# Three sample stages rewritten: index scores by pairs of batches, forget scores and values in column tiles, rings of caches, unrolled loops

## The reference, cut to what matters

```python
# index scores (8 heads of 64 share one key of 64): group A keeps its top 256 keys by them
dots  = einsum('bthd,bsd->bths', iq, ik_all) * 64 ** -0.5
score = einsum('bth,bths->bts', iw * 8 ** -0.5, relu(dots))
sel_score, sel = top_k(score, 256)
# group A: 8 heads on 2 KV heads, softmax over the selected keys with a bias by position
# group B, "forget" attention: 8 heads with keys of their own
logits = einsum('bthd,bshd->bhts', q, k_all) * 64 ** -0.5
logits = logits + (f_q[..., :, None] - f_k[..., None, :])   # cumulative sums of log forget
out    = einsum('bhts,bshd->bthd', softmax(mask(logits)), v_all)
```

## Time and profile before

| | us |
|---|---|
| median of 3 executions (4905.27 to 4925.78) | 4916.42 |
| the profiled execution, its own time | 4921.45 |
| its span in the trace | 4919.4 |
| the index stage, from 2258 to 2460 of the span | 202 |
| the forget stage, 2460 to 2892 | 432 |
| the sparse stage, 2892 to 3093 | 201 |

### The profile page before, as it was taken

The page is one execution under the profiler, slowest core; times in us unless marked ns, Lnnn a source line. Parts: engine busy times, 40 slices in busy tenths (PEclk is TensorE's granted clock), DMA queues, the critical chain, the costliest instruction groups (busy, mean ns, idle before and its releaser), DMA issues. The chain is left out here.

```text
span 4919.4 us, 56872 instructions
## 1 busy us (share of the span) xinstructions
PE 4268.2 (87%) x20062; PEld 3271.9 (67%) x20062; DVE 2392.9 (49%) x4716; ACT 2009.3 (41%) x3516; POOL 188.4 (4%) x224
## 2 busy tenths in 40 slices
PE   7997979997577888898789967797999999999998
PEld 6897967776334444442244535687989898989887
DVE  5322247776587777851134522343434352525354
ACT  4111126665576777752222312223334242424243
POOL 0000000000110000000000000010000000000000
PEclk9998989998688889897689978898999999999999
DMA  4344353331411010001165447565444354444454
GB/s 135 100 135 122 118 151 78 78 78 34 109 49 44 24 39 20 20 7 28 29 205 190 141 109 147 165 204 175 154 137 168 127 169 135 146 155 151 148 163 146
DMA packets 478509, 557.84 MB, mean 113 GB/s; under 512 B 95433, under 2 KB 388177, under 8 KB 473981
## 3 DMA queue, kind: packets, MB, share of 16 engines
q1 hardware_dynamic: 461122, 497.73, 33.3%
q0 software_dynamic: 17120, 56.65, 4.0%
HBM read 444.45 MB, written 109.83 MB: 113 GB/s over the span
## 5 line engine op out<-in xcount | busy, mean ns | idle before, releaser
L2199 DVE TENSOR_TENSOR w_lo<-w_raw,w_hi 128x2048 fp32r<-128x2048 f32 x192 | 440.2, 2293 | 643.3 <-ACT w_hi L2164 629.2
L2164 ACT CAST w_hi<-w_raw 128x2048 fp32r<-128x2048 f32 x192 | 366.7, 1910 | 568.1 <-PE ps_y L2149 541.1
L2128 PE MATMUL ps_u<-h_hi,w_hi 128*128 128x384 f32 (+1 forms) x1536 | 505.9, 329 | 48.9 <-DMA h_lo<-h2lo 27.0
L2130 PE MATMUL ps_u<-h_hi,w_lo 128*128 128x384 f32 (+1 forms) x1536 | 503.4, 328 | 0.0
L2129 PE MATMUL ps_u<-h_lo,w_hi 128*128 128x384 f32 (+1 forms) x1536 | 503.3, 328 | 0.0
L2147 PE MATMUL ps_y<-w_hi,hid_hi 128*128 128x512 f32 x1088 | 423.5, 389 | 0.6 <-DVE w_lo L2199 0.4
L2149 PE MATMUL ps_y<-w_hi,hid_lo 128*128 128x512 f32 x1088 | 423.4, 389 | 0.0
L2148 PE MATMUL ps_y<-w_lo,hid_hi 128*128 128x512 f32 x1088 | 423.3, 389 | 0.0
L332 PE MATMUL ps_u<-hT_hi,wi_hi 128*128 128x436 f32 (+1 forms) x920 | 341.7, 371 | 46.7 <-DVE o_lo L494 29.9
L334 PE MATMUL ps_u<-hT_hi,wi_lo 128*128 128x436 f32 (+1 forms) x920 | 335.9, 365 | 0.0
L333 PE MATMUL ps_u<-hT_lo,wi_hi 128*128 128x436 f32 (+1 forms) x920 | 335.7, 365 | 0.0
(11 more groups left out here) (261 smaller groups left out, 8209.7 us busy)
## 6 DMA issues: line engine op xcount, KB each, us to landing
w_raw<-in_w_up SPq DMA_DIRECT2D x96, 1024.0 KB, 5.3
w_raw<-in_w_down SPq DMA_DIRECT2D x96, 1024.0 KB, 4.9
k_rows_b<-in_cache_b_k SPq DMA_DIRECT2D x32, 1024.0 KB, 11.9
v_rows_b<-in_cache_b_v SPq DMA_DIRECT2D x32, 1024.0 KB, 5.3
part_hi<-o_hi SPq DMA_DIRECT2D x68, 218.0 KB, 2.0
part_lo<-o_lo SPq DMA_DIRECT2D x68, 218.0 KB, 2.2
wi_raw<-in_w_in SPq DMA_DIRECT2D x18, 512.0 KB, 4.3
mx<-mixed SPq DMA_DIRECT2D x17, 512.0 KB, 6.5
```

The lines of the kernel that those rows point to most:

```text
L2128: pe.matmul(out, w_hi[s][:, c], h_hi[:, k, 0:w], start=(k == 0), stop=False)
L2130: mm = pe.matmul(out, w_lo[s][:, c], h_hi[:, k, 0:w], start=False, stop=(k == KD - 1))
L2164: act.copy(w_hi[i % 2][:, :], raw[i % RAW][:, :]).then_inc(ev("w_hi"), 1)
L2199: nc.vector.tensor_tensor(w_lo[i % 2][:, :], raw[i % RAW][:, :], w_hi[i % 2][:, :].bitcast(FP32), ALU.subtract)\
```

## The change

Four things are done, all in the two functions. `need` and the hardware loops go: the batches are written out one by one.

*Index stage.* Two batches form a pair. Their keys lie side by side in one tile, so one transposition turns both; the first batch's keys come to partitions 0 to 63 and the second's to 64 to 127, and the two score products of a chunk use the two halves of TensorE's rows and two PSUM banks. The second product writes 32 columns at partition 0, 32, 64 or 96 (a column tile). All small loads for the 8 batches, 27 DMAs, come ahead of the first score. The keys of each pair have a tile of their own. The forget sums are taken after the third pair and are stored in two parts, high and low, as float32r.

The second batch's queries and mask are now issued after two quarters of the first batch's values, no longer behind all of them. The diff, cut to its core:

```diff
 def sample_index_phase(nc, ctx, d):
...
-        kT = sb("ikT_s", [HD, LS])
+        kn = [sb(f"ik_rows{i}", [P, NBLK, 2, HD]) for i in range(NPR)]
+        kT = [sb(f"ikT_s{i}", [P, PAST]) for i in two]
...
+            def score(pr, c):
+                c0, w = SCH[c]
+                u = NSC * pr + c
+                if c < G:
+                    pe.wait_ge(ev("kT_ready"), G * pr + c + 1)
+                if u >= 2:
+                    pe.wait_ge(ev("relu_ready"), 2 * (u - 1))
+                for a in two:
+                    r = slice(a * HD, (a + 1) * HD)
+                    keys = kT[pr % 2][r, c0:c0 + w] if c < G else kTn[r, pr, :]
+                    pe.matmul(ps_k[u % 2][a][:, 0:w], q[r, pr, :], keys, start=True, stop=True).then_inc(ev("qk_done"), 1)
+
+            def weigh(pr, c):
...
+                for a in two:
+                    j = SLOT * (2 * (c % 2) + a)
+                    pe.matmul(ps_w[n % 2][j:j + SLOT, 0:w], wsel[:, 2 * pr + a, :], relu[u % 2][a][:, 0:w], start=True, stop=True).then_inc(ev("w_done"), 1)
...
+            for pr in range(NPR):
+                for c in range(NSC):
+                    score(pr, c)
+                    if c < G and pr + 1 < NPR:
+                        turn(pr + 1, c)
+                    if c:
+                        weigh(pr, c - 1)
+                weigh(pr, NSC - 1)
+                if pr == LF_AFTER:
+                    forget()
...
 def sample_attend_phase(nc, ctx, d, sparse):
...
+            def load_small(b):
+                p = b % 2
+                if b >= 2:
+                    sp.wait_ge(ev("qk_done"), NSC * (b - 1))
...
+                if b >= 2:
+                    sp.wait_ge(ev("pv_done"), NSC * (b - 1))
+                sp.dma_start(vn[p][0:DS, :], d[f"s_{cache}_v"][b * DS:(b + 1) * DS, :]).then_inc(ev("vn_in", p), 16)
...
+            for n in range(NQ4):
+                load_v(n)
+                if n % 4 == 1 and n // 4 + 1 < DB:
+                    load_small(n // 4 + 1)
+                if n + NKQ < NQ4:
+                    load_k(n + NKQ)
...
                     for i in range(NC):
-                        mm = pe.matmul(out, q[:, i * P:(i + 1) * P], kT[:, i, c0:c0 + w], start=(i == 0), stop=sparse)
+                        own = slice(0, P) if sparse else slice(i * PAIR, (i + 1) * PAIR)
+                        keys = kTn[p][:, i, :] if newest else kT[:, i, c0:c0 + w]
+                        mm = pe.matmul(out[own, 0:w], q[p][:, own], keys, start=True, stop=sparse)
                     if not sparse:
-                        mm = pe.matmul(out, hsel[:, :], nfk[:, c0:c0 + w], start=False, stop=not newest)
+                        mm = pe.matmul(out[:, 0:w], hsel[:, :], nfk[p][:, c0:c0 + w], start=False, stop=not newest)
...
-                        mm = pe.matmul(ps_o[:, 0:W], pT[0:r, kb, :], v[0:r, kb, :], start=(kb == 0), stop=(kb == NBLK))
+                        for j in range(NC):
+                            own = slice(0, P) if sparse else slice(j * PAIR, (j + 1) * PAIR)
+                            mm = pe.matmul(ps_o[own, 0:P], pT[:, kb, own], rows[:, j * P:(j + 1) * P], start=(kb == 0), stop=(kb == NBLK))
```

More of the change, by code:

```diff
@@ new lines, in _ @@
+            for pr in range(NPR):
+                for m in range(3):
+                    take(pr, m)
+                if pr == LF_AFTER:
+                    dve.wait_ge(ev("ones"), 1)
+                    dve.wait_ge(ev("lfT_ready"), G + 1)
+                    nc.vector.tensor_tensor_scan(cum[:, :], ones[:, :], lfT[:, :], 0.0, ALU.mult, ALU.add).then_inc(ev("cum_ready"), 1)
+                    dve.wait_ge(ev("cum_ready"), 1)
+            nc.vector.tensor_scalar(nf_hi[:, :], cum[:, :], -1.0, None, ALU.mult).then_inc(ev("nf_hi"), 1)
@@ L1510, in sample_index_phase @@
+            for p in two:
+                pool.wait_ge(ev("sw_st_sc", p), 16 * 6 * NPR // 2)
     return ev
@@ L1547, in sample_attend_phase @@
         if sparse:
-            mask = sb("mask", [P, LS])
+            mask = [sb(f"mask{i}", [P, LS]) for i in two]
             near = sb("near", [P, WIN])
@@ L1620, in _ @@
+            sp.wait_ge(ev("zeroed"), 1)
+            load_small(0)
+            for n in range(2, NKQ):
+                load_k(n)
+            if not sparse:
+                sp.dma_start(score[:, :], d["sc_s"][:, :]).then_inc(ev("const_in"), 16)
+            for n in range(NQ4):
[4 more added lines that the diff above has]
+                    load_k(n + NKQ)
             if not sparse:
@@ L1684, in values @@
                 weigh(NSC - 1)
+            pe.wait_ge(ev("ident_in"), 16)
             turn_keys(0)
-            scores(0)
-            turn_keys(1)
-            values(0)
-            with pe.Fori(1, DB - 1) as b:
+            pe.wait_ge(ev("const_in"), NCONST)
+            pe.wait_ge(ev("zeroed"), 2)
+            for b in range(DB):
                 scores(b)
-                turn_keys(b + 1)
+                if b + 1 < DB:
+                    turn_keys(b + 1)
                 values(b)
-            scores(DB - 1)
@@ L1695, in _, with keys @@
-            values(DB - 1)
         @block.scalar
         def _(act):
-            def keys(b):
-                need(act, ev("qk_done"), NSC * b)
-                for g in range(G):
-                    act.wait_ge(ev("k_turned"), G * b + g + 1)
+            def keys(b, g0, g1):
+                if b and g0 == 0:
+                    act.wait_ge(ev("qk_done"), NSC * b)
+                for g in range(g0, g1):
+                    u = G * b + g
+                    act.wait_ge(ev("k_turned"), u + 1)
```

489 lines of the change are left out of this document (261 added, 228 removed).

## The result

The changed kernel takes 4599.6 us (median of 4 runs, 4596.1 to 4604.1) for 4916.4: the ratio is 0.9356 (95% interval 0.934 to 0.9372), some 317 us less where the forecast was 182. The profiled execution has a span of 4595.5 us (its own time 4597.5). Sign and range held; the size didn't. The time is not among those that the forecast gave its own case (4690 to 4800); it lies in the range because the range took in most of the way to the rival "all at once" (4571).

What follows compares the result with a forecast made beforehand. TensorE was taken to bound the index and forget stages, with mask waits in the sparse stage. Savings 67 + 80 + 35 = 182 took 4921.45 to 4739; the median, 5 us under the profiled execution, was forecast at 4735 us, range 4570 to 4870.

Steps and rivals of the forecast that it cites:

- its own case: Whole kernel: column tiles overlap in part, clock partly lower; 182 us saved, 4690 to 4800 us, chance 0.38.
- all at once: Rival, forget stage: all four column tiles work together, a chunk's passes take 0.86 us; kernel 4571 us, chance 0.17.
- staircase: Logit chunk on four column tiles: passes start in program order, neighbouring tiles overlap; 8 passes take 5 steps, 2.15 us.
- The two passes of a product stand together in the queue: TensorE's queue: a tile's second pass waits for its first, so only the next tile's first pass runs beside it.
- The forget pass: Forget logits: the forget product becomes one pass, 0.2 us for 0.86; a chunk is 2.15 + 0.55 us.
- part-array products don't hold the upper level: TensorE's clock: products on 64 rows or 16 columns fall to the lower level; index chunk 5.0 us, logits 18.
- First score: Start of the index stage: 27 small DMAs issued ahead put it near 28 us, before 17.
- all at once and upper: Index stage: products overlap fully at the upper clock; stage 92 us, 110 saved.
- its rival 26: Forget period if all four tiles overlap: VectorE's queue ends at 20, logits 5 behind it; 193 us saved.
- SyncE's rings: Rival, forget stage: loads queued behind the new values' load come late, period stays near 51; 4805 us, chance 0.03.
- DMA is as late: 16 us: Sparse stage: DMA needs 16 us a batch at full share, beside a 15.5 us chain; period taken as 17.
- Loops written out: Whole kernel: written-out loops cost instruction fetches, but other such stages stream at full pitch; charged nothing.

Runs made afterwards that it cites:

- index_one_half: The changed kernel, but both index-stage scores of a pair of batches use the first half of the array's rows; 4645.0 us.
- start_finish: The changed kernel with 8 query loads on ScalarE's queue, 8 weight loads on GpSimd's, and VectorE finishing each batch behind two chunks of the next; 4576.0 us.

## Why the prediction was right in sign and short by 135 us

- **Column tiles (the mis-sized term).** The forecast put a staircase of 2.15 us between 3.4 and 0.86; measured 0.97. "The two passes of a product stand together in the queue" was argued from order alone. In the index scores the semaphore steps (the signals that a product is done) of both halves' products stand with the two later passes, so there the first passes of both run together and then the second; for the four tiles of a logit chunk the trace shows two groups of four, not which pass each holds. The Trainium skill (TensorE: Matmul & The Clock Gate, Part 3) has tiles side by side and products in program order; the side by side holds here, 3.6 times as fast for four (3.5 / 0.97), and the trace doesn't say in which order the passes stood in the queue. Values: 10 us forecast, 7.0 measured; logits 18, now 6.7. The forget pass has two sizes in the forecast, 0.2 in one sentence and up to 0.55 in the sum of a chunk; it takes 0.43.
- **The clock (the second).** I read from the earlier trace rows that part-array products don't hold the upper level and took half of the index chunks and of the logits at the lower. The runs show them hold it: 32 columns in turn 17.6 us at 1.00, half rows in turn 10 us at 1.00. What half rows in turn did not do in three pairs of index_one_half is raise it from 0.50; with both halves at work it rose within the first pair and stayed at 1.00. In the logits of the period shown it didn't fall. It is the pairing that the change brings, and I charged it the price of before.
- **Index stage.** First score forecast near 28 us into it, measured 30.2 (2284.2 - 2254): SyncE's issues, right, and start_finish bears the cause out (14.5 us for 23.5). A chunk 5.0 us forecast, 2.63 measured, nearly all of the missing 42 us (16 full chunks by 2.4); the "all at once and upper" line of the text, 92 us, is near the 93 measured, in part by luck: the first pair still ran mostly at the lower clock, and the scan cost TensorE about 3 us for the 4 charged.
- **Forget stage.** Forecast period 41, its rival 26, measured 24.8. The rival named VectorE as next; it is, by 1.8 us at full clock, with TensorE's loop behind it. SyncE's rings blocked nothing: TensorE waits for no load in the loop.
- **Sparse stage.** 35 us forecast, 22 to 23 came: a period of 18.7 for 17, and 1.5 of 4 us at the start. The step "DMA is as late: 16 us" took a mean share for a price; the mask's load slows whatever lies beside it. With that gone the period is 15.7. No run undoes the mask's earlier issue alone, so what it gained is argued.
- **At nothing.** Loops written out: no cost shows; the stages outside sum to the same within 1 us.
- **The range.** Two mechanisms of the forecast's own case were wrong, in the same direction; that the time lay in the range is owed to the rival that it took in, not to the forecast.

## What to carry to other kernels

When a product uses a part of TensorE's array, price its partner before its own passes: four quarters in one queue worked 3.6 times as fast here as in turn, two halves 1.8 times, and a half alone also left the clock at its lower level for most of its stage. Ask of a low clock whether the products lost it or only failed to raise it after a wait. Before a shared resource is called the bound, take half of it away: here a DMA share of 1.02 was worth nothing in one stage, while in another a load that reads 16 rows eight times cost 24 us at a share near 1. Compare single periods at the same clock before a mean of seven. And where limits lie this close (VectorE 24.8, the loop 23.0), one move gives 1 to 2 us.

## What was unexpected of the hardware

- Eight passes on four column tiles start as two groups of four, 0.43 us apart, so a float32 product's two passes were no obstacle here.
- 32 columns in turn kept the clock at 1.00 for 17.6 us. 64 rows in turn stayed at 0.50 for three pairs with TensorE busy throughout, and at 1.00 for 10 us once 16 transposes had raised it.
- A 1 MB load whose 128 rows are 16 rows eight times over moves at some 150 GB/s with all that lies beside it, 8 packets in flight at a time; from 128 rows of its own it lands in 5.3 us. Out of SBUF, eight copies of 16 partitions took 8.7 us to issue, and their packets 1.27 us each.
